# Two blocks of a transformer on one core: modulation weights moved and grouped by columns, attention by pairs of heads

## The reference

```python
sh1, sc1, g1, sh2, sc2, g2 = split(silu(c) @ w_ada + b_ada, 6)          # c, c_ctx: two vectors; w_ada 1024 x 6144
hl = modulate(rmsnorm(h_lat, norm_mix), sh1, sc1)
...
h_lat = h_lat + g1 * merge_branches(...)
h_lat = h_lat + g2 * hier_moe(modulate(rmsnorm(h_lat, norm_ffn), sh2, sc2), ...)

# second block, 8 heads of each kind, over all 512 tokens
w = softmax(q @ k.T * scale);  out = w @ v                              # o_mla; o_dil the same with a mask added
mixed = concatenate([rms_norm(o_mla, g_out_mla), rms_norm(o_dil, g_out_dil)])
h = h + mixed @ w_out
```

## Time and profile before

| | us |
|---|---|
| median of 3 runs | 3506.13 |
| lowest and highest run | 3501.59, 3506.4 |
| the profiled execution | 3473.59 |
| its span, first to last instruction | 3471.6 |

### The profile page before, as it was taken

One profiled execution on the slowest core, in us unless ns is written; L12 is line 12 of the kernel. 1 busy time (PEld: TensorE's weight loads), 2 busy tenths in 40 slices (PEclk: granted clock), 3 DMA queues, 4 the chain that ended last, 5 costly groups with the idle time before them and its releaser, 6 DMA issues. The chain is left out here.

```text
span 3471.6 us, 35875 instructions
## 1 busy us (share of the span) xinstructions
PE 3083.6 (89%) x11536; PEld 1821.1 (52%) x11536; DVE 1598.3 (46%) x3312; ACT 509.9 (15%) x1071; POOL 766.3 (22%) x688
## 2 busy tenths in 40 slices
PE   8998799989987589877889889689999999999986
PEld 1444644446434323323447568587567777776553
DVE  0123500103011312121234329988998878887772
ACT  2122310001101011122125321100000000000002
POOL 0000000000000011110000001155766556556650
PEclk9899899999998699988989999857999999999998
DMA  7201012120123888751300024257999999999992
GB/s 304 99 25 50 1 49 90 62 82 13 73 97 143 327 338 323 314 227 54 117 13 1 1 80 133 86 186 243 352 368 390 362 363 363 364 362 371 410 364 103
DMA packets 156221, 668.47 MB, mean 193 GB/s; under 512 B 22115, under 2 KB 31587, under 8 KB 140771
## 3 DMA queue, kind: packets, MB, share of 16 engines
q1 hardware_dynamic: 73540, 383.09, 29.0%
q0 software_dynamic: 81792, 281.07, 21.6%
q10 hardware_dynamic: 800, 3.15, 0.2%
HBM read 689.25 MB, written 35.65 MB: 209 GB/s over the span
## 5 line engine op out<-in xcount | busy, mean ns | idle before, releaser
L2262 PE MATMUL ps<-wring,pm_weighted 128*128 128x512 f32 x1024 | 474.6, 607 | 34.0 <-DVE pm_weighted L2364 33.9
L346 PE MATMUL ps<-hT,wring 128*128 128x512 f32 (+2 forms) x1232 | 468.8, 543 | 16.3 <-PEq L505 4.9
L2236 POOL DMA_INDIRECT pm_ring<-in_peer_u,pm_idxs x256 | 329.5, 1287 | 172.2 <-DVE pm_dots L2377 89.4
L346 PEld LDWEIGHTS ps<-hT,wring 128*128 128x128 f32 (+1 forms) x1232 | 235.9, 192 | 246.1 <-issue 237.3
L2245 PE MATMUL ps<-hT,wring 128*128 128x256 f32 x1536 | 352.7, 383 | 0.5 <-DMA wring<-in_peer_v 0.5
L2431 DVE SCALAR_TENSOR_TENSOR pm_acc<-pm_ring,pm_coefs,pm_acc 128x1024 f32<-128x1024 f32 x256 | 317.7, 1283 | 59.6 <-DMA pm_ring<-in_peer_v,pm_idxs 59.0
L2236 POOL DMA_INDIRECT pm_ring<-in_peer_v,pm_idxs x256 | 297.9, 1164 | 143.6 <-DVE pm_acc L2431 59.8
L2254 PEld LDWEIGHTS ps<-pm_onehot,hT 128*128 128x128 f32 x2048 | 293.1, 225 | 49.4 <-issue 48.3
L2262 PEld LDWEIGHTS ps<-wring,pm_weighted 128*128 128x128 f32 x1024 | 192.8, 193 | 240.1 <-issue 188.8
L2245 PEld LDWEIGHTS ps<-hT,wring 128*128 128x128 f32 x1536 | 286.8, 190 | 50.0 <-issue 14.4
L1304 POOL COPY ex_idx<-row_token 128x1 uint32 (+1 forms) x24 | 4.4, 184 | 1349.9 <-PEq L1417 1157.8
(11 more groups left out here) (418 smaller groups left out, 3256.6 us busy)
## 6 DMA issues: line engine op xcount, KB each, us to landing
ex_gu<-in_experts SPq DMA_DIRECT2D x48, 2048.0 KB
wring<-in_peer_v SPq DMA_DIRECT2D x128, 512.0 KB, 7.1
ex_dn<-in_experts SPq DMA_DIRECT2D x48, 1024.0 KB
wring<-in_peer_uT SPq DMA_DIRECT2D x96, 512.0 KB, 5.7
wring<-in_w_in SPq DMA_DIRECT2D x21, 2048.0 KB, 7.8
wring<-in_w_ada SPq DMA_DIRECT2D x12, 2048.0 KB, 7.8
pk_u<-in_peer_uT SPq DMA_DIRECT2D x32, 512.0 KB, 3.8
y_dram_out<-gates SPq DMA_DIRECT2D x1, 12288.0 KB, 32.3
```

The costliest lines, as they stand in the source:

```text
L346: mm = env.nc.tensor.matmul(out, w[:, k, lo:hi], rhs(k), start=(k == 0), stop=(k == KD - 1))
L2236: nc.gpsimd.indirect_dma_start(ring[:, r, :], None, dram[table], bass.IndirectOffsetOnAxis(ap=idx[:, half, r:r + 1], axis=0)).then_inc(got ...
L2262: mm = nc.tensor.matmul(env.ps[:, OUT[n], :], W[:, s % 2, t * P:(t + 1) * P], vr[s][:, half * WBLK:(half + 1) * WBLK], start=False, stop=stop)
```

## The change

1. w_ada leaves the ring. `stage_modulation` loads blocks 0 to 3 into four buffers of their own at once, x and ctx are issued at the head of ScalarE's queue, and SP's queue then loads the first two ring blocks.
2. A vector product works on 32 columns of weights (two real, thirty zero) in four column groups: group g sums two of the eight k-tiles into partitions 32g to 32g+31. The columns are then picked out, and the four groups summed, by matmuls with a selection matrix (N = 2) instead of transposes.
3. Blocks 4 to 11 are handled in the gla branch stage by `LateModulation`: three buffers, loads on SP's queue between those of the ring, one vector product after each m projection, and the columns, the second norm's gain and the gates after the fourth y projection.
4. `stage_attention` goes through 32 steps, two heads of one kind and 128 queries each. The weights are normalized before their transpose, the values are multiplied with features as rows (two heads in two column groups of 64, 128 queries moving), VectorE applies the gain straight into `mixT`, and ScalarE squares the same product into `sq` (laid over hT).
5. `stage_mix` and the following `stage_out` become `stage_attention_out`: one product per kind, scaled by the token's inverse root while it is added to h. The sums of squares come from 32 matmuls with one moving column of ones.
6. Some buffers (gla's mask and squares, the memory stage's accumulator) are laid over `gates`, and constants grow by one load.

```diff
+def vector_times_block(env, pe, t, w):
+    bank_ready(env, pe, t)
+    for i in range(KD // KG):
+        for g in range(KG):
+            k = KD // KG * g + i
+            mm = env.nc.tensor.matmul(env.ps[32 * g:32 * g + 32, t[0], :], env.silu_c[:, k, :], w[:, k, :],
+                                      start=(i == 0), stop=(i == KD // KG - 1))
+    mm.then_inc(env.bank_full[t[0]], 1)
...
@@ stage_modulation, SP, then TensorE
+                for n in range(ADA_FIRST):
+                    nc.sync.dma_start(w[:, n, :], dram["w_ada"][n]).then_inc(w_in[n], 16)
...
                 load_blocks(env, sp)
...
+                for j in range(16):
+                    mm = nc.tensor.matmul(env.ps[:, t_col[0], 2 * j:2 * j + 2], row[:, j * P:(j + 1) * P],
+                                          env.sel[:, P:P + 2], start=True, stop=True)
...
+class LateModulation:
...
+    def load(self, sp, first, last):
...
+        for n in range(first, last):
+            if n >= 3:
+                product_done(env, sp, self.tiles[n - 3])
+            nc.sync.dma_start(self.w[:, n % 3, :], env.dram["w_ada"][ADA_FIRST + n]).then_inc(self.w_in[n % 4], 16)
...
+    def columns_on_tensor(self, pe, t_col, t_bc):
...
+        for j in range(32):
+            mm = nc.tensor.matmul(env.ps[:, t_col[0], 2 * j:2 * j + 2], self.row[:, j * P:(j + 1) * P],
+                                  env.sel[:, P:P + 2], start=True, stop=True)
...
+            nc.tensor.matmul(env.ps[:, t[0], :], env.sel[:, 0:P], self.row[:, at:at + WBLK], start=True, stop=False)
+            nc.tensor.matmul(env.ps[:, t[0], :], env.ones[0:1, :], self.brow[0:1, i * WBLK:(i + 1) * WBLK],
+                             start=False, stop=True).then_inc(env.bank_full[t[0]], 1)
...
@@ stage_branch, SP, then TensorE
+                if late:
+                    late.load(sp, 0, 3)
+                    load_blocks(env, sp, until=b_m[1] + 1)
+                    late.load(sp, 3, 6)
+                    load_blocks(env, sp, until=b_y[0] + 1)
+                    late.load(sp, 6, ADA_LATER)
...
+                            if late and tl is m_t:
+                                late.block_on_tensor(pe, 4 * i + j)
...
+                    if late and i == 1:
+                        late.columns_on_tensor(pe, t_col, t_bc)
...
@@ stage_attention, VectorE, end of a step
+                        for a in both:
+                            nc.vector.tensor_scalar(pr[:, u % 3, a, :], pr[:, u % 3, a, :], inv[:, u, a:a + 1], None,
+                                                    ALU.mult).then_inc(nrm_s, 1)
+                    if s >= 3:
+                        u = s - 3
+                        kind, hp, qt = steps[u]
+                        v.wait_ge(sq_s, u + 1)
+                        nc.vector.tensor_scalar(mixT[:, 4 * kind + hp, qt * P:(qt + 1) * P], env.ps[:, pv[u][0], 0:P],
+                                                col(env, "g_mla", 4 * kind + hp), None, ALU.mult).then_inc(
+                            env.bank_free[pv[u][0]], 1)
...
@@ stage_attention, ScalarE, a step: two exponentials of s, two copies of s - 2, then
+                    if s >= 3:
+                        u = s - 3
+                        kind, hp, qt = steps[u]
+                        product_done(env, act, pv[u])
+                        nc.scalar.activation(sq[:, 4 * kind + hp, qt * P:(qt + 1) * P], env.ps[:, pv[u][0], 0:P],
+                                             ACT.Square).then_inc(sq_s, 1)
...
@@ stage_attention, TensorE, a step: two scores of s, eight transposes of s - 2, then of s - 3
+                        for kt in range(NT):
+                            for a in both:
+                                hd = 2 * hp + a
+                                mm = nc.tensor.matmul(env.ps[VH * a:VH * (a + 1), pv[u][0], 0:P],
+                                                      val[:, kt, hd * VH:(hd + 1) * VH],
+                                                      pt[:, u % 2, a, kt * P:(kt + 1) * P],
+                                                      start=(kt == 0), stop=(kt == NT - 1))
...
@@ stage_attention_out, VectorE, then TensorE
+                            nc.vector.scalar_tensor_tensor(env.h[:, i, cs], env.ps[:, t[0], :], iv[:, i, kind:kind + 1],
+                                                           env.h[:, i, cs], ALU.mult, ALU.add).then_inc(
...
+                                        mm = nc.tensor.matmul(env.ps[:, t_ss[0], 2 * u + kind:2 * u + kind + 1],
+                                                              sq[:, 4 * kind + k, u * P:(u + 1) * P], env.ones[:, 0:1],
+                                                              start=(k == 0), stop=(k == KD // 2 - 1))
```

More of the change, by code:

```diff
@@ L111, in evacuated, with load_blocks @@
     eng.wait_ge(env.bank_free[t[0]], t[1] + 1)
-def load_blocks(env, sp, ahead=2):
+def load_blocks(env, sp, ahead=2, until=None):
     nc = env.nc
-    for b in range(env.issued, min(env.used + ahead, len(env.blocks))):
+    for b in range(env.issued, min(env.used + ahead, len(env.blocks)) if until is None else until):
         if b >= 2:
@@ L700, in stage_branch @@
     b_g = [env.take_block(g_t[3]), env.take_block(g_t[7])]
-    m_t = env.tiles(8)
+    m_t = []
+    for j in range(8):
+        m_t.append(env.tile())
+        if late:
+            late.tiles.append(env.tile())
     b_m = [env.take_block(m_t[3]), env.take_block(m_t[7])]
-    y_t = env.tiles(8)
+    y_t = env.tiles(4)
+    t_col, t_bc = (env.tile(), env.tiles(4)) if late else (None, None)
+    y_t += env.tiles(4)
     b_y = [env.take_block(y_t[3]), env.take_block(y_t[7])]
@@ L727, in _ @@
                     nc.vector.tensor_tensor(oT[:, j, :], oT[:, j, :], gate[:, j, :], ALU.mult).then_inc(mul_s, 1)
+                if late:
+                    for n in range(ADA_LATER):
+                        late.block_on_vector(v, n)
                 for j, t in enumerate(y_t):
+                    if late and j == 4:
+                        late.columns_on_vector(v, t_col, t_bc)
                     product_done(env, v, t)
@@ new lines, in _ @@
+                        for a in both:
+                            bank_ready(env, pe, sc[s][a])
+                            if kind == 0:
+                                q, k = M.q[:, 2 * hp + a, qs], M.k[:, 2 * hp + a, :]
+                            else:
+                                half = slice(DH * a, DH * (a + 1))
+                                q, k = M.dqk[half, hp, qs], M.dqk[half, 4 + hp, :]
+                            nc.tensor.matmul(env.ps[:, sc[s][a][0], :], q, k, start=True, stop=True).then_inc(
+                                env.bank_full[sc[s][a][0]], 1)
@@ L1830, in _ @@
+                    if s >= 3:
+                        u = s - 3
+                        kind, hp, qt = steps[u]
+                        for a in both:
+                            evacuated(env, pe, tr[u][a])
                         bank_ready(env, pe, pv[u])
@@ new lines, in _ @@
+                for half in range(2):
+                    cs = slice(half * WBLK, (half + 1) * WBLK)
+                    for i in range(NT):
+                        for kind, t in enumerate(tl[half][i]):
+                            product_done(env, v, t)
+                            if kind:
+                                evacuated(env, v, tl[half][i][0])
+                            nc.vector.scalar_tensor_tensor(env.h[:, i, cs], env.ps[:, t[0], :], iv[:, i, kind:kind + 1],
+                                                           env.h[:, i, cs], ALU.mult, ALU.add).then_inc(
+                                env.bank_free[t[0]], 1)
@@ L2532, in first_mixer @@
     yT = branch.enter_context(nc.sbuf_tensor("yT", [P, KD, S], F32))
-    stage_branch(env, "gla", oT, yT, True)
+    with ExitStack() as own:
+        stage_branch(env, "gla", oT, yT, True, LateModulation(env, own, "ada2"))
     with ExitStack() as own:
```

375 lines of the change are left out of this document (201 added, 174 removed).

## The result

The changed kernel takes 3403.68 us (median of 4 runs, 3391.41 to 3413.92), the kernel before 3503.86 beside it (4 runs, 3489.06 to 3506.40). The ratio is 0.9721, 95% interval 0.9676 to 0.9767, thus 98 us less (82 to 114; the medians are 100 apart). The forecast was 3432 with a range of 3410 to 3468: the sign and most of the mechanism came as forecast, the gain was larger, and the time lies 6 us under the low end.

A forecast was written before the change was run, and what follows sets the result against it. TensorE was taken to bound the start, the gla branch stage and the attention. The terms, -81 + 38 - 30 - 1 = -74, took the profiled 3473.6 us to 3400, or 3432 as the median; range 3410 to 3468.

The forecast's parts named there:

- the new ring: Attention loop: VectorE's mixT waits for ScalarE's Square, ahead of the next row maxima; period 3.64 us plain, 4.02 masked.
- rival 1: Vector products: four column groups run only two at a time, 3.5 us a block; 3446 us in all, chance 0.15.
- rival 3: Vector products and attention: no overlap among 32-column groups; 3489 us in all, chance 0.05.
- rival 2: Attention: ring slower or TensorE at 4.3 us, 3445; lower clock in gla branch and output, +9 more; chance 0.14.
- rival 4: Attention: each step closes before the next begins, 8.1 us a step; slower than before, 3569 us, chance 0.03.
- the prediction's signs of being wrong: Vector products taking 3.5 or 6.9 us, attention period over 4.3, or column matmuls dragging the clock of what follows.
- Step A: Start: only 4 of 12 modulation blocks stay ahead of the first norm, which starts at 43 us; -81 (-85 to -74).
- Step B: Gla branch stage: the other 8 modulation blocks are paid in full on TensorE; +38 us (31 to 55).
- I take 10: Gla branch stage: eight 512-column matmuls for the gates, 16 instructions, taken as 10 us (7 to 15).
- Step C: Attention by pairs of heads: 32 steps of mean 3.83 us, 127.6 against 157.5 us; -30.
- Step D: Mix and output stages: 71 against 72.2 us; -1 (-6 to +2).
- I take the difference over as it is: Whole kernel: the profile's 32.5 us below the 3506.1 median carried over, 3400 for a profile, 3432 as median.

The follow-up runs named there:

- e6: Changed kernel with the gates' eight products ahead of the 32 column matmuls; 3402.19 us, ratio 0.9745 to the kernel before.
- e9: Changed kernel with the gates' bias loaded to all 128 rows and added by VectorE, without the single-row products; 3400.11 us in one run.
- e7: Changed kernel with the attention's mixT done one step later, between the row maxima and the normalization; 3394.57 us, ratio 0.9720 to the kernel before.
- e1: The kernel before once more, without an edit; 3496.27 us in 12 runs, ratio 1.0003.
- e3: Changed kernel with the attention, mix and output stages of the kernel before, so the modulation part alone; 3452.92 us, ratio 0.9877 to the kernel before.
- e8: The kernel before with the change's constant added as an unused input array; 3493.99 us, ratio 0.9998.
- e2: The changed kernel again, without an edit; 3400.37 us, ratio 0.9724 to the kernel before.
- e12: The changed kernel a third time, without an edit; 3412.43 us, ratio 0.9761 to the kernel before.
- e11: Changed kernel with later mixT, gates' bias on VectorE, gate products ahead of the columns and sums of squares spread; 3376.99 us, ratio 0.9677 to the kernel before.
- e10: Changed kernel with the 64 single-column instructions for the sums of squares cut into 32, 16 and 16 between output products; 3389.12 us in one run.

## Why the prediction was right, and where it fell short

**Most of the mechanism held.** TensorE bounds the branch stage and the plain steps of the attention, the new ring most of the masked steps, and nothing became a bound that the prediction hadn't named. None of the rivals came as a whole: a block takes 1.92 and not 3.5 (rival 1) or 6.8 (rival 3), the period is 3.81 and at most 4.02 and not over 4.3 (rival 2), and no step closes before the next begins (rival 4). One part of rival (2) did come, the lower clock in B, and with it one of the prediction's signs of being wrong: the column matmuls dragged the clock of what follows them, the gates.

**Step A, right.** Norm at 43 forecast, 43.56 measured (39.8 to 44.0 in the other profiles with this start); fourth block landed at 31 and 31.60; column matmuls 7.1 and 6.96.

**Step B, right in sum, one term mis-sized.** +38 forecast, +41.7 measured (169.3 to 211.0 us for the stage). Vector products 16 forecast, 15 measured (8 x 1.86 from start to start); columns 10.7 and 9.3, losing the clock on the way as forecast, though that half of them would run at each level stood in no row. The mis-sized term is "I take 10" for the gates: 16.0, over its upper bound of 15. It took a value between the two levels of the clock, but the columns ahead had already taken the clock down, the single-row products didn't bring it back, and each pair of them cost 0.2 to 0.3 us over its instructions (e6, e9). The bounds of the step were also added up wrongly: its terms give 29 to 58, not 31 to 55.

**Step C, right in sum, by a partly different working.** 127.6 forecast, 127.9 measured. The ring's 4.02 came out exactly for the masked steps in which the ring has closed, and e7 shows that it was the ring. The forecast has it for all 16 and 3.64 for the plain ones, mean 3.83; the measured mean of eight steps is 3.81, since the first of each masked group takes 3.11 and the plain ones take 3.81. That the two differences cancel is luck. For the plain kind the prediction has the ring's 3.64 above TensorE's 3.45. In fact TensorE's step is 3.81: 1.82 for four score instructions (4 x 0.427 = 1.71), 0.97 for the transposes (0.87) and 1.02 for the values (0.86). TensorE is the bound there, by its own work and 0.1 to 0.16 us at each of three changes of the kind of matmul, which the prediction had put into a slack of TensorE that these steps don't have. Two dilated scores do run beside each other (4 instructions in 1.06), which is why e7 gets to 3.11; in the changed kernel the ring takes most of that back.

The prediction weighed the skill's rule that changing the tiling mode drains TensorE (the Trainium skill, TensorEngine Tiling (Array Packing), section Key Properties) and put it under 0.1 us a change. These runs agree with the rule, at a higher price: 0.1 to 0.16 in the attention, 0.2 to 0.3 for two changes between 128 rows and one; that the time goes into a drain is not shown. By the other rule that it weighed, the 2.38x of the Trainium skill for three column tiles (TensorE: Matmul & The Clock Gate, section Part 3), four groups would lose a fifth, as an estimate. They lose less: 16 instructions take 1.86 from start to start where 16 x 0.427 / 4 = 1.71 is the ideal, 92% of it, and that with two changes of mode in it.

**Step D, right.** -1 forecast, -2.2 measured. The sums cost 11.4, not 10.7.

**So the changed stages hold -70.3 between the two profiles, forecast -74.** The miss lies elsewhere.

**The step that failed: "the stages that change hold no part that I can tie this to, so I take the difference over as it is".** The profiled execution lay 32.5 under the median, and the prediction kept the same distance for the changed kernel. In fact its profile lay 10 us above its median. The 3506.1, of three runs, was itself high for this kernel, whose medians in the later comparisons are 3489 to 3496. Three things are behind it.
(1) The memory stage varies from one execution to the next, in both kernels alike: 868.1, 893.7 and 883.3 in three profiles of before (mean 881.7), 888.3, 871.8 and 888.7 in three of after (mean 882.9). The profile of before had the fastest. It is TensorE's weighted products that vary, and the waits for VectorE beside them, and the granted clock goes with both. The four of all 14 profiles in which the stage takes 868 to 872 us have the clock at its lower level for 123 to 130 us of it, the other ten, with 878 to 894, for 143 to 164. Groups of instructions, of before:

```profile
L2262 PE MATMUL ps<-wring,pm_weighted 128*128 128x512 f32 x1024 | 474.6, 607 | 34.0 <-DVE pm_weighted L2364 33.9
```

and of e1, the same kernel:

```profile
L2262 PE MATMUL ps<-wring,pm_weighted 128*128 128x512 f32 x1024 | 493.6, 627 | 42.2 <-DVE pm_weighted L2364 42.0
```

(columns: busy us, mean ns of one, idle us before them and what ended it). 19 us of busy time and 8 of waiting go with it. Between the two the stretches at the lower clock differ by 41 us, and half of that is lost work if TensorE is busy: 20 us, an estimate that fits the 19. Why the clock falls more often in one execution than in another stays open.
(2) A stage that does change has such a part too. The stretch at the lower clock at the old attention's start lasts 13.7 us in before and e3, and 30.7 in e1 and e8, which then cost 10 more. The new one has 6.8 us in every profile, and takes 204.9 to 205.2 in all that have it unaltered. So the change is worth 38.4 and not 32 there on the mean of before, e1 and e8 (243.4 to 205.0), and some 37 with e3, on the mean of four (241.7). One profile couldn't show that, but the lower clock at the attention's start was in it to be read, and what the changed kernel does with such a start should have been a term.
(3) Router, experts and expert sum, which nobody touched, are faster behind the modulation change: 71.6 to 72.0 for the router against 73.2 to 74.0, 54.1 to 54.5 for the sum against 55.5 to 55.8, 346.0 to 350.4 for the experts against 348.6 to 356.2. Some 3 us are sure, up to 7 possible. The prediction had nothing for it. The 3 us lie in two waits for the DMA: from the norm's last evacuation to the router's first product it takes 5.0 to 5.2 us instead of 6.4 to 7.0 (the slowest store of the normed tokens lands within 4.9 us instead of 5.6 to 6.8), and the gathered rows of the expert sum are there 18.6 to 19.0 us after the last expert product instead of 20.0 to 20.3. An added input array doesn't do it (e8). Why the DMA lands sooner stays open.

**The account.** All but the memory stage: 2603.5, 2612.0 and 2609.6 in before, e1 and e8, mean 2608.4; 2523.8, 2527.5 and 2525.8 in after, e2 and e12, mean 2525.7. The difference is -83. The ratios gave -98, -96 and -83, -92 on average. The 10 us between are not explained. Three intervals of 10 to 16 us to each side leave some 8 to each side for their mean, an estimate, and the parts of -83 vary by 8 among the profiles of before alone. The memory stage is hardly tied to the change: its mean is 882.5 in the four profiles with the old modulation and 879.8 in the ten with the new. By the -83 the median would have been 3423 from the 3506 that was given, inside the range. What put the time below it is the rest, of runs that lie apart by more than the range allowed for.

**The range.** It was built from the bounds of the terms alone: its low end of 3410 is 3506 less the best of every term (-97). The runs went past that end although the terms came out near their middle, so it wasn't the terms that the range lacked room for. A single kernel's executions lie 45 us apart (e1), and a comparison of four runs with four had an interval of 16 us to each side. That spread belonged on both ends, beside the bounds of the terms: the three runs shown, 3501.6 to 3506.4, made it look like 5, though the profile at 3473.6 said otherwise.

## What to carry to other kernels

Where the profiled execution lies well off the median of the runs, find the stage that holds the difference before the sum is carried over, and put that distance into the range on both sides; the granted clock of each stage is the first thing to compare, above all of one which starts at the lower level. A vector product of 32 columns in four column groups costs a little over a quarter of its instructions' time (1.92 of 6.83 us), in both orders that were tried, so what is dear in moving it is what surrounds it: the small matmuls that turn rows to columns lose the clock, and single-row products that add a bias should go to the engine that reads the product out. In a loop of three engines, write down the ring that goes through the last operation of a step and put that operation behind the ones which another engine waits for: it was worth 14 us here. And before a gain of one stretch is counted, add the stretch behind it: a low clock that is only moved saves nothing (e11 beside e9).

## What the runs showed of the hardware beside this

- Matmuls of 128 rows and of one row in turn cost 1.05 us for two instructions at full clock and 2.0 at half, where 0.85 and 1.71 are their own time (e6, after). The clock did not come back in 16 us of them in after, but did behind eight instructions of 128 rows (e9).
- Matmuls with one or two moving columns cost 0.11 us an instruction at full clock (32 in 3.50 from start to start, e10) and 0.216 at half (13.81 us for 64, e6). A long row of them takes the clock down: behind one piece of 64 it is low for 13.7 us, with pieces of 32 and 16 for 3.4 (e10).
- The same instructions in the same order run at the lower clock for 13.7 us in two executions and for 30.7 in two others (before and e3, e1 and e8).
- One kernel's executions take 3473 to 3519 us, and the mean granted clock goes from 0.923 to 0.912 with them (e1).
